# A top-2 expert stage whose products become three products of split parts, with fill rows skipped in the gather and results scattered to token order

## The reference

```
gp = softmax(x @ w_group_router); g_w, g_idx = top_k(gp, 1)          # 1 of 4 groups
top_w, top_i = top_k(softmax(el_of_group), 2)                        # 2 of its 4 experts
hid = silu(x @ w1[e]) * (x @ w3[e])                                  # 1024 -> 256
out = sum over the 2 experts of gate * (hid @ w2[e])                 # 256 -> 1024
x = x + gt2 * rmsnorm(out, g_post_ffn)
```

## Time and profile before

| | |
|---|---|
| median of 3 runs | 2101.04 us (2100.4 to 2104.65) |
| the profiled execution | 2096.08 us, of which its span is 2094.2 |
| TensorE busy | 1889.6 us, 90% of the span |
| VectorE, ScalarE, GpSimd busy | 793.5, 588.8, 166.4 us |
| mean granted TensorE clock | 0.946 |
| HBM traffic | 291.64 MB read, 38.11 MB written |
| indirect DMAs (queue q0) | 28.32 MB |

### The profile page before, as it was taken

One profiled execution on the slowest core, in us unless ns is written; L12 is line 12 of the kernel. 1 busy time (PEld: TensorE's weight loads), 2 busy tenths in 40 slices (PEclk: granted clock), 3 DMA queues, 4 the chain that ended last, 5 costly groups with the idle time before them and its releaser, 6 DMA issues.

```text
span 2094.2 us, 29812 instructions
## 1 busy us (share of the span) xinstructions
PE 1889.6 (90%) x12396; PEld 1570.3 (75%) x12396; DVE 793.5 (38%) x1415; ACT 588.8 (28%) x930; POOL 166.4 (8%) x192
## 2 busy tenths in 40 slices
PE   6799898999999997999938998989999999959992
PEld 2798555779999974888718975557799998747881
DVE  3312556753223445111172226477523234431113
ACT  2310351652122320111152203516522123201113
POOL 0102410000000000010040033100000000001001
PEclk8899999999999998999958999999999999969996
DMA  9113442212122528999772123021111324269994
GB/s 354 62 56 84 152 143 83 100 42 80 61 71 92 191 81 313 351 354 358 282 255 86 54 62 134 32 91 62 61 61 61 101 69 184 91 227 357 355 344 171
DMA packets 191347, 322.94 MB, mean 154 GB/s; under 512 B 9672, under 2 KB 121608, under 8 KB 190984
## 3 DMA queue, kind: packets, MB, share of 16 engines
q1 hardware_dynamic: 171176, 262.05, 36.3%
q10 hardware_dynamic: 12288, 31.02, 4.3%
q0 software_dynamic: 7776, 28.32, 3.8%
HBM read 291.64 MB, written 38.11 MB: 157 GB/s over the span
## 4 chain that ended last, share of the span: by engine, by line
PE 81%; DVE 10%; ACT 3%; issue 3%; DMA 3%; POOL 0%; SPq 0%; POOLq 0%; DVEq 0%; ACTq 0%
PE pair L1749 71%; PE opair L1749 6%; PE pair L1831 3%; DVE mid L1299 1%; DMA ring<-in_w_mod 1%; PE pair L1771 1%; DVE r L1588 1%; DMA r<-h_rows,ids 1%; ACT r L1051 1%; ACT r L1015 1%; ACT ysT_r L775 1%; DMA ysT<-expert_out,ids 1%; DVE mid L1311 1%; DVE r L1623 0%; DVE hT L1452 0%
## 5 line engine op out<-in xcount | busy, mean ns | idle before, releaser
L1749 PEld LDWEIGHTS pair<-r,ring 128*128 128x128 f32 x2176 | 252.6, 195 | 18.7 <-issue 15.3
L1749 PE MATMUL pair<-r,ring 128*128 128x128 f32 x2176 | 253.1, 278 | 2.6 <-DVE r L1584 2.6
L1749 PE MATMUL pair<-hT_r,mid_r 128*128 128x320 f32 x768 | 237.3, 309 | 0.0
L1749 PE MATMUL pair<-r_r,ring_r 128*128 128x320 f32 x832 | 211.8, 309 | 2.7 <-DVE ring_r L1184 2.7
L1749 PE MATMUL pair<-ysT_r,mid_r 128*128 128x256 f32 (+1 forms) x768 | 170.6, 313 | 14.7 <-issue 9.5
L1831 PE MATMUL pair<-cst,mid 128*128 128x128 f32 x748 | 119.2, 300 | 70.0 <-DVE mid L1130 37.5
L1749 PE MATMUL pair<-mid_r 128*128 128x320 f32 x576 | 178.9, 311 | 1.6 <-issue 1.6
L1831 PEld LDWEIGHTS pair<-cst,mid 128*128 128x128 f32 x748 | 92.2, 152 | 116.5 <-DVE mid L1130 45.1
L1749 PE MATMUL pair<-r_r,mid_r 128*128 128x256 f32 (+2 forms) x576 | 179.3, 311 | 0.0
L1749 PE MATMUL pair<-mid_r,ring_r 128*128 128x320 f32 x576 | 178.0, 309 | 0.0
L1749 PEld LDWEIGHTS pair<-r_r,ring_r 128*128 128x128 f32 x832 | 145.7, 188 | 3.3 <-DVE ring_r L1184 3.3
(11 more groups left out here) (254 smaller groups left out, 3159.1 us busy)
## 6 DMA issues: line engine op xcount, KB each, us to landing
ring<-in_w_mod SPq DMA_DIRECT2D x23, 2048.0 KB, 8.4
ring<-in_w_gate SPq DMA_DIRECT2D x34, 1024.0 KB, 7.3
ring<-in_w_up SPq DMA_DIRECT2D x34, 1024.0 KB, 12.5
ring<-in_w_down SPq DMA_DIRECT2D x34, 1024.0 KB, 11.1
ring<-in_w_in SPq DMA_DIRECT2D x24, 1024.0 KB, 6.7
expert_out<-r ACTq DMA_DIRECT2D x34, 512.0 KB, 7.3
ring<-in_w_in SPq DMA_DIRECT2D x8, 2048.0 KB, 11.0
ring<-in_w_branch SPq DMA_DIRECT2D x12, 1024.0 KB, 5.2
```

The costliest lines, as they stand in the source:

```text
L1749: return nc.tensor.matmul(out, lhsT, rhs, start=first, stop=last, skip_group_check=True)
```

## The change

The expert products become `three_products`. For each block ScalarE rounds and VectorE subtracts: both weight halves, the down weights, the transposed tokens, and the hidden values. The up product now has the tokens as stationary operand and 512 columns of weights (gate and up side by side) as moving one, so its result has one row per token, and the hidden values are transposed by TensorE (`turn_hidden`) before down. Down(b-1) stands behind up(b) now, where down(b) stood behind it. The first two and last two blocks are written out, and the loop runs over the pairs between.

Fill rows carry a number outside the bound, and both the gather and a new indirect scatter skip such rows; the scatter writes result rows to `expert_out` by token (2 x 640 rows). SP reads them back with one plain DMA per token tile (1 MB). Zeroing is gone. SP's load order at the start is: gate and up of block 0, of block 1, down of block 0.

The other edits: several layer-start semaphores are merged into one (`resumed`), a memset of `xg` on GpSimd stands ahead of the list of rows, and VectorE has five more small steps in that list.

```diff
+        w13_parts = [(view(mid_r, s * 4096, 4096), view(ring_r, (1 - s) * 6144, 4096)) for s in range(2)]
+        w2_parts = [(view(ysT_r, s * 2048, 2048), view(ring_r, (1 - s) * 6144 + 4096, 2048)) for s in range(2)]
...
+                for t in range(TT):
+                    sp.dma_start(picks[t], expert_out.rearrange("(k t p) d -> p t k d", k=2, p=P)[:, t]).then_inc(picked[t], 16)
...
-                        for w, at_ in ((w_gate, 0), (w_up, 2048)):
-                            sp.dma_start(w13[s][:, at_:at_ + 2048].rearrange("p (k f) -> p k f", k=KD),
-                                         w[ds(L * NE + e, 1)].rearrange("a (k p) f -> p (a k) f", p=P)).then_inc(up_in[s], 16)
-                        sp.wait_ge(y_filled, it * 2 + (s + 1))
...
+                def load_pair(b):
+
+                    load_up(b + 2, 0)
+                    load_down(b + 1, 1)
+                    load_up(b + 3, 1)
+                    load_down(b + 2, 0)
...
+                def round_up(s, rnd):
+
+                    for i, signal in enumerate((gate_in, up_in)):
+                        act.wait_ge(signal[s], rnd * 16 + 16)
+                        nc.scalar.copy(w13_parts[s][0][:, i * 2048:(i + 1) * 2048], w13[s][:, i * 2048:(i + 1) * 2048]).then_inc(rounded, 1)
...
+                def block_rounds(b, s, rnd, first, last):
+
+                    gate_values(b, s)
+                    if not (last and s):
+                        round_tokens(b + 1, 1 - s)
+                    round_down(s, rnd)
+                    round_hidden(b, s)
+                    if not (first and s == 0):
+                        store_block(b - 1, 1 - s, rnd - 1 + s)
+                    if not last:
+                        round_up(s, rnd + 1)
...
+                def block_remainders(b, s, last):
+
+                    hidden(b, s)
+                    if not (last and s):
+                        remainder_tokens(1 - s, b * 5 + 6)
+                    remainder_down(s, b * 5 + (4 if last and s else 7))
+                    remainder_hidden(s, b * 5 + (5 if last and s else 8))
+                    if not last:
+                        remainder_up(s, b * 5 + 9)
...
+                    pool.indirect_dma_start(xg[:, s, :], None, h2_rows, bass.IndirectOffsetOnAxis(ap=src_id[s], axis=0),
+                                            bounds_check=T - 1, oob_is_err=False).then_inc(xg_in[s], 16)
...
+                    pool.indirect_dma_start(expert_out, bass.IndirectOffsetOnAxis(ap=row_id[s], axis=0), yo[:, s, :], None,
+                                            bounds_check=2 * T - 1, oob_is_err=False).then_inc(yo_stored[s], 16)
...
+                def up(b, s):
+
+                    pe.wait_ge(t_freed, b + 2)
+                    pe.wait_ge(down_ready, b + 1)
+                    pe.wait_ge(w13_ready, b * 2 + 2)
+                    w = [x.rearrange("p (j k f) -> p k j f", j=2, k=KD) for x in w13_parts[s]]
+                    for k in range(KD):
+                        last = three_products(pair[1][:, s * 512:(s + 1) * 512], [x[:, k * P:(k + 1) * P] for x in xg_parts[s]],
+                                              [x[:, k] for x in w], k == 0, k == KD - 1)
...
+                def block(b, s, rnd, first, last):
+
+                    up(b, s)
+                    if not (last and s):
+                        gathered(b + 1, 1 - s, rnd + s)
+                    if not (first and s == 0):
+                        down(b - 1, 1 - s)
+                    turn_hidden(b, s)
```

More of the change, by code:

```diff
@@ L466, in bass_hybrid_step @@
         picked = [sem(f"picked{i}") for i in range(TT)]
+        gate_in = [sem(f"gate_in{i}") for i in range(2)]
         up_in = [sem(f"up_in{i}") for i in range(2)]
+        rounded, w13_ready, w2_ready = sem("rounded"), sem("w13_ready"), sem("w2_ready")
+        hid_turned, down_ready = sem("hid_turned"), sem("down_ready")
         down_in = [sem(f"down_in{i}") for i in range(2)]
@@ L1048, in _ @@
-                with act.Fori(0, n_pairs) as it:
-                    for s in range(2):
-                        act.wait_ge(h_filled, it * 2 + (s + 3))
-                        nc.scalar.activation(sil[:, s, :], pair[1][:, s * 512:s * 512 + FF], ACT.Silu).then_inc(sil_ready, 1)
-                        act.wait_ge(y_filled, it * 2 + (s + 3))
-                        act.wait_ge(yo_stored[s], it * 16 + 16)
-                        nc.scalar.copy(yo[:, s, :], (pair[2], opair)[s][:, :]).then_inc(y_read, 1)
-                        act.wait_ge(y_read, it * 2 + (s + 4))
-                        act.dma_start(out_blocks[ds(it * 2 + s, 1)].rearrange("a p d -> p (a d)"), yo[:, s, :]).then_inc(yo_stored[s], 16)
+                await_read(act, ("list", 0))
@@ new lines, in store_block @@
+                def store_block(b, s, rnd):
+                    act.wait_ge(y_filled, b + 3)
+                    if not isinstance(rnd, int) or rnd:
+                        act.wait_ge(yo_stored[s], rnd * 16)
+                    nc.scalar.copy(yo[:, s, :], (pair[2], opair)[s][:, :]).then_inc(y_read, 1)
+                for i in range(2):
+                    act.wait_ge(h2_stored[i], 16 * ((TT + 1 - i) // 2))
+                round_up(0, 0)
+                round_tokens(0, 0)
+                round_up(1, 0)
@@ L1058, in _ @@
+                with act.Fori(0, n_more - 1) as it:
+                    for s in range(2):
+                        block_rounds(it * 2 + (4 + s), s, it + 2, False, False)
+                for s in range(2):
+                    block_rounds(n_more * 2 + (2 + s), s, n_more + 1, False, True)
+                store_block(n_more * 2 + 3, 1, n_more + 1)
                 if not last_layer(L):
@@ L1591, in _ @@
[L1591 to L1601 removed]
+                dve.sem_inc(down_ready, 2)
@@ new lines, in remainder_up, with remainder_down @@
+                def remainder_up(s, count):
+                    for i in range(2):
+                        own = slice(i * 2048, (i + 1) * 2048)
+                        dve.wait_ge(rounded, count + i)
+                        V.tensor_tensor(w13_parts[s][1][:, own], w13[s][:, own], w13_parts[s][0][:, own], ALU.subtract).then_inc(w13_ready, 1)
+                def remainder_down(s, count):
+                    dve.wait_ge(rounded, count)
+                    V.tensor_tensor(w2_parts[s][1], w2s[s], w2_parts[s][0], ALU.subtract).then_inc(w2_ready, 1)
@@ L1604, in _ @@
+                for s in range(2):
+                    block_remainders(s, s, False)
+                with dve.Fori(0, n_more) as it:
+                    for s in range(2):
+                        block_remainders(it * 2 + (2 + s), s, False)
+                for s in range(2):
+                    block_remainders(n_more * 2 + (2 + s), s, True)
                 if not last_layer(L):
@@ new lines, in _ @@
+                for b in range(4):
+                    gather(b, b % 2)
+                    gather_rows(b % 2, b + 1)
+                with pool.Fori(0, n_more) as it:
+                    for s in range(2):
+                        gather(it * 2 + (4 + s), s)
+                        gather_rows(s, it * 2 + (5 + s))
+                        scatter(it * 2 + s, s)
+                        scatter_rows(s, it * 2 + (1 + s))
+                for i in range(4):
+                    scatter(n_more * 2 + i, i % 2)
+                    scatter_rows(i % 2, n_more * 2 + (i + 1))
@@ L1734, in _ @@
-                for t in range(TT):
-                    pool.wait_ge(picked[t], 32)
                 pool.dma_reset()
```

265 lines of the change are left out of this document (140 added, 125 removed).

## The result

The changed kernel takes 2089.59 us (median of 5 runs, 2088.31 to 2091.32) against 2101.04 (median of 5 runs, 2099.49 to 2104.65): a ratio of 0.9943, 95% interval 0.9931 to 0.9955. It gains 11.5 us where 26 were forecast. The profiled execution has a span of 2087.0 us, 7.2 less than before.

The account below looks back on a forecast made before the run. It took DMA traffic to bound the changed expert loops, at periods of 10.7 and 10.9 us. Starts, loop and last steps gain 30.9 us, layer ends lose 5: -26 from 2101.0 gives 2075, 80% range 2058 to 2097.

Parts of the forecast that it names:

- the loop through one weight buffer: Expert loops: two block periods last at least one buffer's release to landing plus 11.7 us, so a period is at least 10.4.
- Landing: Weight buffer's release until its new up weights land: near 9.2 us, from 5.2 for a lone load, 2.95 and about 1.
- Chain: From landing to the end of up: rounding, subtraction, hidden product, token remainder, up and signals, 11.7 us.
- the traffic: Expert loops: with fill rows skipped, DMA engines at 355 GB/s need 10.5 us per block in layer 0, 10.7 in layer 1.
- lock or in-order waits: Rival, 0.19: GpSimd index operations hold VectorE to 10.8 us per block, plus 0.4 of landing waits; period 11.2, 2087 us.
- Slower: Rival, 0.10: release to landing stays at 12.5 us, two periods are 24.2, 2112 us; it decides from 11.9.
- Fill rows not saved: Rival, 0.05: an out-of-range index still costs its 4 KB, so a block stays 4.19 MB, period 11.8, 2104 us.
- Faster traffic: Rival, 0.15: DMA engines reach 375 GB/s in the loops, so the buffer loop's 10.4 us binds; 2064 us.
- Start: First blocks of each layer: up(0) ends later, 842.9 against 840.9, but up(2) earlier; gain 0.6 us, layer 1 0.8.
- Middle: Loop steps: 15 in layer 0 gain 16.1 us, 13 in layer 1 gain 11.4; the last steps gain 2 together.
- Ends: After each layer's last up: results ready 8.3 us later, second tile read at 23; loss 1.5 and 3.5, 5 together.
- Zeroing, list steps, table load: Layer 0's zeroing was called hidden behind attention, four more VectorE list steps (about 0.8 us) hidden behind the weights.

Follow-up runs that it names:

- down_small: Changed kernel with only 256 of 2048 columns of the down weights loaded, rounded and subtracted eight times over: 2097.2 us, with 18 blocks in layer 1 instead of 16.
- hold_gate: Changed kernel with the down weights of b+1 asked for only when the gate half of b+2 has landed: 2089.65 us.
- warm: Changed kernel with TensorE making the eight token transposes twice, 1.04 us more work a block: 2085.59 us.
- short_sub: Changed kernel with VectorE subtracting only 16 of 2048 columns of the up half, all loads whole: 2070.62 us.
- ileave: On top of early, silu and hidden product of b+1 stand ahead of the up half of b+2: 2070.9 us.
- khalf_norel: khalf, but both halves of the weights are asked for only when up has ended: 2065.56 us.
- khalf: ileave with up weights loaded and split in two halves of rows; up starts on the first, whose buffer is released in the middle of up: 2061.41 us.
- fill_gather: Changed kernel with fill rows gathered again instead of skipped, the scatter still skipping them: 2089.51 us.
- early: Changed kernel with the token work of b+2 (transposes, rounding, subtraction) moved ahead of its up weights: 2084.04 us.

## Why the prediction went wrong

**The step that failed is "the loop through one weight buffer", and with it the choice of 10.7 and 10.9 for the period.** I had the formula, two periods are landing plus chain, and gave it 9.2 + 11.7 = 20.9, half of it 10.4, below the traffic's 10.5; so I let the traffic set the pace, with 0.2 on top for the two limits taking turns. Both terms were too small, and in place of that 0.2 it was 0.6 to 0.7:
- Landing: 10.1 in layer 0 and 10.5 in layer 1. I added the second megabyte and a share of gather and scatter to the lone load of the earlier trace rows, but not the down load, which SP issues 3.6 us after the release (932.47, after 928.84). With seven eighths of it gone the landing is at 9.3 (down_small), my figure. That it comes late because the down load is issued ahead of it isn't shown: hold_gate issued that load later, and the landing stayed at 10.2.
- Chain: 12.3. Rounding and subtraction were as priced (4.2), hidden product and token remainder with their signals too (1.7). Up took 5.9 at full clock, from its start to the next load's issue, and 6.4 on average, since 8 of 24 ups ran slow. I had named the TensorE clock below 1.00 as a thing that would make me wrong, and had not priced it. At full clock the chain is 11.8, close to my 11.7. But the slow clock isn't what held the period: almost without it (hold_gate's seven blocks, warm) the landing came later, at 10.2 and 10.5, and layer 0's period was 11.2 all the same.

That half of 10.1 + 12.3 is the 11.2 measured is bookkeeping and proves nothing. What shows the loop at work are the edits: with all the traffic left in, 2.1 us less of subtraction (short_sub) or 1.6 us less of waiting behind it (ileave) takes 0.5 us off each block of layer 0, and with a start on half of the weights as well (khalf_norel) it is 0.8. What I had wrong beyond the sizes is that I compared two limits as if the larger alone counted. The landing depends on how full the DMA engines are, so near the traffic's figure both add to the period; what the landing is made of stays open.

**The traffic** was about right as a bound: 10.2 and 10.5 per block in khalf and 10.6 and 10.9 in ileave (layers 0 and 1), at a share of 0.99 to 1.02, against a forecast of 10.5 and 10.7. The changed kernel just didn't reach it: 0.95 and 326 GB/s. Skipping fill rows saved the bytes forecast, but the gather's part of it no time here (fill_gather).

**Rivals.** The time landed at "lock or in-order waits" (2087), with its period of 11.2. That the number fits is partly luck, for the case reached it by VectorE at 10.8 us a block, which didn't happen; the in-order waits did. The waits are there: silu and tokens behind a weight landing; ileave, which reorders only these, gives 19 us. The lock isn't: VectorE's 68 subtractions of weights took 2281 to 2297 ns, 2293 in the median, against 2284 on average before, with GpSimd's index operations beside them. GpSimd waits for VectorE, and not the other way round; one scatter of the loop at 1.02 us with the subtraction that began after it, one at 2.88:

```profile
935.65 1.02 POOL L1851 DMA_INDIRECT expert_out<-r,ids  x1 [0.88 <-POOL ids L1845]
936.05 2.29 DVE L1664 TENSOR_TENSOR ring_r<-ring,mid_r 128x2048 fp32r<-128x2048 f32 x1 [1.00 <-ACT mid_r L1072]
...
947.36 2.88 POOL L1851 DMA_INDIRECT expert_out<-r,ids  x1 [0.88 <-POOL ids L1845]
```

The second one is issued within the subtraction from 947.05 to 949.34 and ends 0.9 us after it. In the two loops twelve index-driven transfers are issued within a subtraction; they take 2.2 to 3.1 us, and each ends 0.9 us after the subtraction does. The Trainium skill's "SBUF — State Buffer", section "Who interferes with whom", has the later of the two wait. The rows agree where the later one is GpSimd's. Where it is VectorE's they don't: 37 times a subtraction begins while GpSimd is at such an issue, as at 936.05, and each takes 2.28 or 2.29 us. GpSimd has slack here, as priced. "Slower" fell since the landing is at 10.1 to 10.5, below its 11.9. "Fill rows not saved" fell by q0. "Faster traffic" was only seen for a while: khalf moves 373 and 365 GB/s in the windows 880:902 and 902:925, then 345 to 354 in those up to 992.

**Start.** Up(0) was to end 24 us after the first gate load (22.0 before, 2 late); it took 26.0. The up half landed 12.1 us after the gate load was issued, at 835.80, and up ran 8.2 instead of 7.0:

```profile
835.80 1.90 ACT L1072 CAST mid_r<-ring 128x2048 fp32r<-128x2048 f32 x1 [3.61 <-DMA ring<-in_w_up]
...
841.33 0.80 PE L1882 MATMUL pair<-mid_r,r_r 128*128 128x512 f32 x1 [5.38 <-DVE hT_r L1674]
```

By the third silu the two starts had lost 2.3 us where I forecast a gain of 1.4.

**Middle.** Forecast -27.5 and -2 for the last steps, came -16.2. This is where most of the missing gain is; the starts have 3.7 us of it.

**Ends.** Forecast a loss of 5, came 2.0: layer 0 lost nothing. The result is ready 8.0 us after the silu (forecast 8.3 after up), the copy, index copy and scatter are as priced, but the second tile is read 7.3 us after SP's first read is issued, not 8.2 or more.

**Zeroing, list steps, table load** were priced at nothing, and nothing is seen of them, but that is no test. Zeroing stood in the stretch ahead of the first gate load, which ends at 818.9 us before and anywhere from 817.6 to 823.7 in executions of the changed prologue; no run took any of the three alone.

## What to carry to other kernels

Write the loop through each buffer as a sum, release to landing and landing to release, and put into the first part every transfer that is issued before the landing, and into the second every instruction that stands in any engine's order between the landing and the release; compare half of it (with two buffers) with each engine's work. Don't take the first part for a constant: it was 9.3 us with the DMA engines at a share of 0.81, 10.1 at 0.95 and 10.9 at 0.99 (down_small, the changed kernel, ileave). Where the sum comes out near the traffic's figure, leave more than 0.2 us for the two together. An edit that merely reorders helps only if the whole chain gets shorter: early moved one piece out and another in, ileave took both out. When a product becomes fast, look for work that can start on half of its data: khalf took another 9 us off ileave, nearly as much as the 11.5 of the faster products themselves.

## What the runs showed of the hardware

- TensorE's granted clock fell after waits, but not after every one. All 8 slow ups of 24 in the changed kernel's loops, which lost 1.6 us each, followed 1.8 to 3.2 us of waiting, and none came without a wait. But the up at 944.37 followed 2.3 us of it at full clock, and hold_gate waited longer in the window 890:990 (11.9 us against 9.9) with the clock at 1.00. Neither the busy share nor the sum of the waits tells them apart; what does stays open. The period was 11.2 with slow ups and without.
- The same prologue has its first transposes anywhere from 45.3 to 49.8 us, and the expert stage of layer 0 starts up to 6 us apart (817.6 to 823.7): a single profiled execution isn't enough for an effect of 5 us.
- 7.3 MB of gathered fill rows, all of one source row, fitted into DMA engines at a share of 0.95 without a change of the time. Skipping those rows saves their bytes but no packets: q0 has 9792 either way.
- An index-driven transfer that GpSimd issued during a VectorE subtraction of two SBUF operands took 2.2 to 3.1 us instead of 1.0; a subtraction that began during such an issue took no longer (37 cases).
